# Hybrid decoder step: two of five expert value sums read the whole value table, and the order of work ahead of the first gather

## The reference, cut to what matters

```python
xn = rmsnorm(x); xr, yr, ca, cb, ga, gb = split(xn @ w_in)          # 2048 x 8192
branch_a = (rglru(conv4(xr)) * gelu(yr)) @ w_a                       # recurrence over time
branch_b = silu(layernorm(conv31(ca * sigmoid(cb)))) @ w_b           # 31 taps, 1024 channels
x = x + (sigmoid(ga) * branch_a + sigmoid(gb) * branch_b) @ w_out
# experts: 16384 of them, 8 heads, 16 of each head for each token
q = (rmsnorm(x) @ w_q).reshape(t, 8, 2, 128)
s1, s2 = q[:, :, 0] . keys1, q[:, :, 1] . keys2                      # 128 scores each
e, sv = top16 of (top16(s1) + top16(s2));  e = i1 * 128 + i2
w = softmax(sv) * gelu(u_tab[e] . xn)                                # one dot product of 2048 for each
x = x + sum over heads and k of w * v_tab[e]                         # u_tab, v_tab: 16384 x 2048
y = rmsnorm(x) * g_final
```

## Time and profile before

| | us |
|---|---|
| median of 3 runs | 4106.34 (4100.68 to 4108.57) |
| the profiled execution | 4110.75 |
| its span, first to last instruction | 4108.9 |

### The profile page before, as it was taken

The page is one execution under the profiler, slowest core; times in us unless marked ns, Lnnn a source line. Parts: engine busy times, 40 slices in busy tenths (PEclk is TensorE's granted clock), DMA queues, the critical chain, the costliest instruction groups (busy, mean ns, idle before and its releaser), DMA issues.

```text
span 4108.9 us, 35344 instructions
## 1 busy us (share of the span) xinstructions
PE 3168.1 (77%) x11808; PEld 1910.2 (46%) x11808; DVE 2447.8 (60%) x3360; ACT 556.5 (14%) x1113; POOL 1543.0 (38%) x1130
## 2 busy tenths in 40 slices
PE   6999899879878776857915777777777777776776
PEld 5999889775444443535502233232223232322322
DVE  2788810146787775784666565566556555656553
ACT  4444320110010000001000100010011001001100
POOL 2000000014554443552336455445445544554442
PEclk9999999889999998978968999999999999999999
DMA  4322367569999998896879999999999999999997
GB/s 122 89 85 84 104 215 242 190 244 344 391 380 387 385 392 343 333 385 253 342 263 406 409 416 421 421 403 421 414 416 417 422 415 415 418 421 412 422 412 306
DMA packets 406321, 1372.39 MB, mean 334 GB/s; under 512 B 24449, under 2 KB 264065, under 8 KB 264735
## 3 DMA queue, kind: packets, MB, share of 16 engines
q0 software_dynamic: 157584, 1145.05, 68.3%
q1 hardware_dynamic: 246382, 221.85, 16.9%
q10 hardware_dynamic: 2257, 4.40, 0.3%
HBM read 1363.20 MB, written 8.86 MB: 334 GB/s over the span
## 4 chain that ended last, share of the span: by engine, by line
DMA 43%; PE 29%; DVE 14%; issue 9%; POOL 4%; ACT 1%; SPq 0%; DVEq 0%; POOLq 0%; ACTq 0%
DMA region<-in_v_tab_dram,region 29%; DMA region<-in_u_tab_dram,region 13%; PE ps L1366 11%; PE ps L1547 6%; POOL region L527 4%; DVE region L1177 3%; PE ps L1349 3%; PE ps L1351 3%; PE ps L1350 3%; DVE region L1230 2%; DVE region L1168 1%; DVE region L1129 1%; DVE region L1126 1%; DVE region L1128 1%; DVE region L1125 1%
## 5 line engine op out<-in xcount | busy, mean ns | idle before, releaser
L1547 PE MATMUL ps<-region,region 128*128 128x512 f32 x3032 | 1429.1, 621 | 544.0 <-DMA region<-in_v_tab_dram,region 326.8
L1366 PE MATMUL ps<-region,region 128*128 128x160 f32 (+1 forms) x5120 | 1237.2, 404 | 190.4 <-DVE region L1065 57.3
L1230 DVE SCALAR_TENSOR_TENSOR region<-region,region 128x2048 f32<-128x2048 f32 x384 | 876.2, 2291 | 738.8 <-DMA region<-in_u_tab_dram,region 738.8
L527 POOL DMA_INDIRECT region<-in_v_tab_dram,region x544 | 764.3, 1405 | 1268.6 <-PE ps L1547 675.8
L1547 PEld LDWEIGHTS ps<-region,region 128*128 128x128 f32 x3032 | 575.8, 197 | 1397.4 <-issue 1304.3
L1366 PEld LDWEIGHTS ps<-region,region 128*128 128x128 f32 x5120 | 861.1, 196 | 558.9 <-issue 104.1
L527 POOL DMA_INDIRECT region<-in_u_tab_dram,region x544 | 740.7, 1362 | 794.3 <-DVE region L1158 341.0
L1177 DVE SCALAR_TENSOR_TENSOR region<-region,region,region 128x2048 f32<-128x2048 f32 x160 | 376.1, 2351 | 236.8 <-DMA region<-in_v_tab_dram,region 236.6
L1168 DVE SCALAR_TENSOR_TENSOR region<-region,region 128x2048 f32<-128x2048 f32 x160 | 365.3, 2285 | 22.8 <-DMA region<-in_u_tab_dram,region 22.8
L1349 PE MATMUL ps<-region,region 128*128 128x272 f32 x1024 | 297.4, 290 | 0.0
L1351 PE MATMUL ps<-region,region 128*128 128x272 f32 x1024 | 296.4, 289 | 0.0
(11 more groups left out here) (202 smaller groups left out, 1483.2 us busy)
## 6 DMA issues: line engine op xcount, KB each, us to landing
region<-in_w_in_dram SPq DMA_DIRECT2D x192, 512.0 KB
region<-in_w_out_dram SPq DMA_DIRECT2D x64, 512.0 KB
region<-in_w_q_dram SPq DMA_DIRECT2D x64, 512.0 KB
region<-in_w_a_dram SPq DMA_DIRECT2D x32, 512.0 KB
region<-in_w_b_dram SPq DMA_DIRECT2D x32, 512.0 KB
region<-in_u_tab_dram,region POOLq DMA_INDIRECT x544, 14.0
region<-in_v_tab_dram,region POOLq DMA_INDIRECT x544, 14.0
region<-in_x_prompt_dram SPq DMA_DIRECT2D x7, 1024.0 KB, 15.7
```

The source lines that it names most:

```text
L527: pool.indirect_dma_start(out=slot, out_offset=None, in_=rows_ap, in_offset=bass.IndirectOffsetOnAxis(ap=idx[:, k:k + 1], axis=0)).then_in ...
L1230: stt(out=u_b[s], in0=u_b[s], scalar=1.0, in1=xn_tile(UNITS_A + u), op0=ALU.mult, op1=ALU.mult, accum_out=dots[u % 2][:, k:k + 1]).then_in ...
L1366: last = mm(outs[n][:, 0:WIDTH[g]], wide[s][:, q, n * P:(n + 1) * P], rhs(k), start=(k == 0), stop=(k == n_k - 1))
L1547: last = mm(acc[n][:, b * 512:(b + 1) * 512], diag[:, m, :], v_b[s][:, b * 512:(b + 1) * 512], start=(m == 0), stop=(m == len(rows) - 1))
```

## The change

1. **Values of tiles 0 and 1 by the whole table.** The 256 value gathers of these tiles (256 MB) are gone. Instead the 128 x 128 weights of each token over (i2, i1) are built, and `v_tab` is read once, 128 chunks of 128 experts (1 MB each); each chunk is multiplied into both tiles: 2 x 4 matmuls of 128 x 128 by 128 x 512.
   - `split_experts` (DVE) splits the indices of a tile in two; `turn` (PE, 3 transposes) and `turned_copy` (ACT) put the 128 (head, k) of a token on the partitions.
   - 32 batches of 4 tokens for each tile: `first_ones` (DVE, 4 instructions: column equals i1, times weight), `second_ones` (ACT, 4 squares of (column - i2) and one Relu(1 - square)), `batch` (PE, 4 products 128 x 128 by 128 x 128), `keep_weights` (ACT, PSUM to SBUF: 512 columns, written 4 together, 128 apart; read 128 apart).
   - Tile 0's batches are spread over rows 136 to 251 of stage B; tile 1's stand at rows 258 to 265 (`BATCH_AT`), 4 at each. On ACT they stand ahead of the next unit's scores.
   - `SP` loads chunk c when chunk c - 2 has been used (2 buffers).
2. **Tile 2** is done last, on VectorE: dot product of row z, then value row z - 18, with 2 buffers for `u_tab` rows and 2 for `v_tab` rows (before: 4 and 4), beside the chunks.
3. **Values of stage A.** Of its 160 value rows 80 stay on VectorE, spread evenly behind the dot products (`VALUE_AT`); the other 80 go to TensorE with diagonal weights, spread over the first 224 rows of stage B (`ROW_AT`), with the 2 buffers of stage A. The last rows of stage A's list end with the queries: 18 rows for the 8 heads (before: 32, and 18 more for the lag behind them).
4. **Scores of group 1** are written to DRAM (3 MB, `scores_kept`) after the last head, since their place is needed; each unit's 128 KB come back through ACT's DMA queue.
5. **Ahead of the first gather:** the last chunk's 31-tap convolution is split by columns (`last_conv`): group 0's 128 prompt columns first, the other 384 in three parts among the norm and merges of group 0, ahead of `norm_mean(1)`; `gate_b(0, 1)` moves ahead of `norm_mean(1)`; the four sums of `xp` (L1074) stand behind `norm_scale(0)`; the clears behind `channels_out(0)` and `route(0)`; the score of group 0's head 0 right behind its own product; two clears on GpSimd at the start behind its first subtraction.

The diff, cut to its core:

```diff
+ROWS_W = 5 * TOPK
+ROWS_1, ROWS_B = 2 * P, 3 * P
+VALUE_AT = {V_LAG + v * (ROWS_A - V_LAG) // ROWS_W: v for v in range(ROWS_W)}
+ROWS_P = ROWS_A - ROWS_W
+ROW_AT = [m * (ROWS_1 - 2 * TOPK) // ROWS_P for m in range(ROWS_P)]
+BATCH = 4
+BATCHES = P // BATCH
+BATCH_AT = [[P + 8 + b * (P - 9) // BATCHES for b in range(BATCHES)],
+            [ROWS_1 + 2 + b // 4 for b in range(BATCHES)]]
...
-    return 142 + 4 * h, 146 + 4 * h
+    return 142 + 18 * h // HEADS, 142 + 18 * (h + 1) // HEADS
...
+            sp.wait_ge(v_used, ROWS_P)
+            for c in range(CHUNKS):
+                if c == 1:
+                    sp.wait_ge(built, 2 * BATCHES)
+                if c >= 2:
+                    sp.wait_ge(vt_used, c - 1)
+                sp.dma_start(v_t[c % 2], v_rows[c * P:(c + 1) * P, :]).then_inc(vt_landed[c % 2], 16)
...
+            for r in range(ROWS_1):
...
+                if r >= SLOTS:
+                    pool.wait_ge(dot_b, r - SLOTS + 1)
+                gather(u_rows, u_b[r % SLOTS], ub_landed[r % SLOTS], idx_all, ROWS_A + r)
+                for m, at_row in enumerate(ROW_AT):
+                    if at_row == r:
...
+                            pool.wait_ge(v_used, m - SLOTS_V + 1)
+                        value_row(ROWS_W + m)
+            for z in range(P + V_LAG + 1):
...
+                    pool.wait_ge(dot_b, r - 1)
+                    gather(u_rows, u_b[2 + z % 2], ub_landed[2 + z % 2], idx_all, ROWS_A + r)
+                v = z - V_LAG - 1
...
+                        pool.wait_ge(v_added, ROWS_W + v - SLOTS_V + 1)
+                    value_row(ROWS_A + v)
...
+            def second_ones(t, b):
+                n = t * BATCHES + b
+                if n >= 2:
+                    act.wait_ge(built, n - 1)
+                for q in range(BATCH):
+                    last = nc.scalar.activation(one_b[n % 2][:, q, :], count, ACT.Square, scale=-1.0,
+                                                bias=turned[:, 1, BATCH * b + q:BATCH * b + q + 1])
+                last.then_inc(b_square, 1)
+                act.wait_ge(b_square, n + 1)
+                nc.scalar.activation(one_b[n % 2], one_b[n % 2], ACT.Relu, scale=-1.0, bias=ones[:, 0:1]).then_inc(b_ones, 1)
...
+            def keep_weights(t, b):
...
+                act.wait_ge(built, n + 1)
+                if t == 0:
+                    nc.scalar.activation(wx[:, :, cols], src, ACT.Copy).then_inc(kept_w, 1)
+                else:
+                    nc.scalar.activation(wy[0][:, :, cols], src[:, 0:HALF], ACT.Copy)
+                    nc.scalar.activation(wy[1][:, :, cols], src[:, HALF:CHUNKS], ACT.Copy).then_inc(kept_w, 1)
...
             norm_center(0)
...
+            last_conv(0, 12, 0, NBT)
             norm_scale(0)
+            join_parts((0, 1, 2, 3))
+            last_conv(12, 18, 0, NBT)
             merge(0, 0)
             merge(0, 1)
+            last_conv(18, CW, 0, NBT)
...
+            for r in range(ROWS_B):
+                u, k = divmod(r, TOPK)
+                dot(r)
+                if k == 1:
+                    expert_weights(UNITS_A + u - 1)
+                if k == (12 if u == 2 * HEADS else 3) and u < UNITS_B - 1:
+                    route(UNITS_A + u + 1)
...
+                if r >= ROWS_1 + V_LAG:
+                    value_z(r - ROWS_1 - V_LAG)
...
+            for c in range(CHUNKS):
+                s = c % 2
+                pe.wait_ge(vt_landed[s], 16 * (c // 2 + 1))
+                for n in range(2):
+                    w = wx[:, c, :] if n == 0 else wy[c // HALF][:, c % HALF, :]
                     for b in range(4):
...
+                        last = mm(acc[n][:, b * 512:(b + 1) * 512], w, v_t[s][:, b * 512:(b + 1) * 512],
+                                  start=(c == 0), stop=(c == CHUNKS - 1))
```

More of the change, by code:

```diff
@@ L97, in steps_query @@
 def steps_query(h):
-    return 142 + 4 * h, 146 + 4 * h
-PE_ROWS = (tuple(range(TOPK)), tuple(k for k in range(TOPK) if k not in SHARED))
+    return 142 + 18 * h // HEADS, 142 + 18 * (h + 1) // HEADS
 class Steps:
@@ L576, in _ @@
[L576 to L588 removed]
+                    value_row(v)
@@ L843, in _, with build @@
+            def build(t, batches):
+                for b in batches:
+                    second_ones(t, b)
+                    if b > batches[0]:
+                        keep_weights(t, b - 1)
+                if batches:
+                    keep_weights(t, batches[-1])
             for j in range(DC):
@@ L1241, in normalised @@
+            def normalised(tiles, n, g):
                 dve.wait_ge(rms_sqrt, n)
@@ new lines, in _ @@
+            for r in range(ROWS_1):
+                for m in range(ROWS_P):
+                    if ROW_AT[m] == r:
+                        value_row(m)
+                if r == SPLIT_AT[0]:
+                    turn(0)
+                for b in range(BATCHES):
+                    if BATCH_AT[0][b] == r:
+                        batch(0, b)
+                if r == FOLD_AT - 3:
+                    pe.wait_ge(acc_read, 2)
+                    for b in range(4):
+                        last = mm(acc[0][0:TS, b * 512:(b + 1) * 512], sel[:, 1, 0:TS], xf[1][:, b * 512:(b + 1) * 512],
+                                  start=True, stop=True)
+                    last.then_inc(fold_done, 1)
```

493 lines of the change are left out of this document (314 added, 179 removed).

## The result

| | us |
|---|---|
| changed kernel, median of 4 runs | 4193.48 (4190.24 to 4202.32) |
| kernel before, on the same chip, median of 4 runs | 4107.45 (4100.68 to 4111.97) |
| ratio | 1.0214, 95% interval 1.0197 to 1.0231 |

The change makes the kernel 2.1% slower, 86 us. The forecast was 4055 us: the sign is wrong and the time is 138 us off. The profiled execution of the changed kernel took 4202.32 us, its span 4200.5.

The account below looks back on a forecast made before the run. Taken as bound by gathers (DMA) in stage B and the branches, by PE in the queries. Sum: 936 + 560 + 230 + 182 + 15 + 944 + 103 + 1063 + 21, 1.85 outside the span: 4056, forecast 4055 us; range 3885 to 4150.

Parts of the forecast that it names:

- step 5: Stage B, tiles 0 and 1: 16 units of 59 us (bounds 53 and 66), 944 us, ending at 2867.
- step 7: Chunks beside tile 2: 1063 us, rows at 8.8 us (bounds 7.5 and 10.5), bound by tile 2's two-buffer loop.
- Step 1: Ahead of the first gather: 3 us off the start of group 1 (936), 11 for the gather.
- Step 2: Group 1's branches: 669 becomes 560 us, pairs of 70 us (bounds 66 and 76).
- Step 3: Output blocks: 268 becomes 230 us (bounds 215 and 250).
- Step 4: Queries: 190 becomes 182 us, the 59 us behind them go, late scores add 15; stage B starts at 1923.
- Step 6: Building tile 1's weights ahead of the chunks: 103 us, 2.8 us a batch (bounds 2.5 and 4.5).
- rival C: Tile 1's build: strided PSUM copies cost three times 0.8 us, build 51 us longer, kernel 4107 us; chance 0.05.
- Step 8: End, from tile 2's last value row: 21 us (15 to 30), against 12.8 before.
- A: Stage B: the DMA queue stays full, units 55 us, tile 2's stretch 980 us, kernel 3909 us; chance 0.3.
- B: Tile 2 beside the chunks: the two-buffer loop takes 10.2 us a row, +87 us, kernel 4143 us; chance 0.2.
- a lasting fall to 1.2 GHz: PE beside tile 2: long waits for chunks drop its clock from 2.4 GHz, a chunk then taking 13.8 us.

Follow-up runs that it names:

- the halves: Changed kernel with each 1 MB value-table chunk loaded and multiplied as two column halves of 512 KB: 4176.99 us, 1.0177 of before.
- the best version: Changed kernel with value gather first, route in three parts, chunks in halves, and tile 0's batches at each unit's 9th, 11th, 13th and 15th row: 3984.11 us.
- the two orders: Changed kernel with the value gather issued ahead of the expert-row gather beside tile 2, and each stage B route in three parts: 4100.97 us.
- all three edits: Changed kernel with value gather first beside tile 2, stage B routes in three parts, and chunks loaded in column halves: 4026.65 us, 0.9801 of before.

## Why the prediction was wrong

The largest misses of the sum are step 5 (+84 us) and step 7 (+63).

**Step 1** (start, 3 us): the start of group 1 moved by 2 us (937.1 for 939). "First gather near 845" was wrong: I followed the moved work to the indices and not to the semaphore that releases the gather, whose instruction waits for ScalarE.

**Step 2** (branches): right, the window 936 to 1500 answers to 560 us. **Step 3** (output blocks): 250 in place of 230, at the upper bound. I had left 24 us above the floors of two engines and read 30 for before; by the prediction's own figures that was 27 above the DMA engines' 241 and 62 above PE's 206, and now it is 44 above both. Neither PE (179.4 busy) nor the DMA engines (0.86) is full. No run took this apart, and the cause stays open. **Step 4** (queries): 185 for 182, so that they ended at 1935, 27 us later than forecast, and PE's wait of 51 us behind them is gone, as forecast. The first unit of stage B then took 83.7 us, 21 more than the others; DVE waits 19.9 us for the first scores to come back from DRAM. I had allowed 15 for that ahead of stage B; it came behind its first rows, and so stage B started only 12 us late.

**Step 5** (units of 59): the mechanism was the right one, the queue that drains during a route, and the run with the route in three parts shows it (57.8). What failed is its size, and with it the sentence on what hides ACT's batches. The idle time is 7.5 us (12% of 62.8) for 6; the refill is slower than I took from the earlier trace rows, where the issue takes 0.94 us: behind a route DVE is busy without a break and the issues on GpSimd take about 2 us. The transfers took some 55 us for 52.8, since in tiles 0 and 1 the engines moved 355 GB/s at a share of 0.88, 403 for a full share, and not 417. And the order of the batches, which I had called covered ("What hides ACT's batches: 4 of 2.7 us for each unit, on an engine busy a tenth"): ACT is idle, but it is idle because it waits, and what stands behind its wait is needed by PE and then by GpSimd. A low busy share was taken for availability. In tile 1 it costs 4.6 us a unit once the route is cut (63.7 to 59.1). The first unit is 25 us of the 84, the other seven of tile 0 are 25, tile 1's eight 34.

**Step 6** (build): 91 us for 103; a batch is 2.46 us for 2.8 (32 of 2.8 are 90 us, not the 91 of the sum), and rival C (the strided copies are dear) is refuted. Tile 0's copies, by form:

```profile
L931 ACT ACTIVATE region<-ps 128x512 f32<-128x512 f32 x32 | 19.1, 597 | 236.3 <-PE ps L1758 236.3
```

512 columns read 128 apart take 0.60 us, while 544 contiguous ones took 0.63; tile 1's copies of 256 take 0.37. The rule of the Trainium skill, "Advanced Engine Details and Errata", section Memory Cachelines, on every two consecutive elements doesn't show in these copies on ScalarE.

**Step 7** (tile 2), 63 us. What failed is the sentence "both are shorter than what I hold for the bound": I priced the chunks by PE's work, 128 x 6.9, and never worked out their own loop of two buffers, though I had done so for the rows. They come every 8.4 us, last 1076 us instead of 900, and so stand beside the rows to the end: the 12 rows at 7.2 don't exist (+21), 98 rows at 8.98 take 880 us and not 860 (+20), the last 18 values 15 us more, the first rows 7.

The run with the halves shows what that error is worth. Its chunks last 897 us, as forecast, and its last 16 rows, behind the chunks, come 7.1 us apart (no route falls in them). The stretch is then 1095.7 us, 31 less than in the changed kernel (the medians differ by 16), and 33 us above the forecast stay: the rows beside the chunks come 9.1 us apart, the first rows take 7 us more and the last values 8. Nor was the 8.8 us of a row forecast for the right reasons. Without chunk loads a row takes 7.90 us, where my loop gave 7.2 (6.7 and 0.5 for the route); the loads add 1.1 us, where I had 1.6. Two errors of opposite sign brought the forecast near the measured 8.98, which is luck.

**Step 8**: 20.3 us for 21.

Of the rivals, A (the queue stays full, 3909) was approached once the order of the work was changed: the best version takes 3984 us, with a share of 0.94 to 1.02 outside the build. B had the right sign and a right place, with a price per row that is not what was measured (10.2; 8.98). Its sum is off too: 26 rows at 7.2 in place of 12 are 101 us more, so B stands at 4157 and not 4143. The kernel came out on B's side because tiles 0 and 1 were late and the chunks slow as well. The two-sided range, 3885 to 4150, missed by 43 us, since it added no lateness in tiles 0 and 1 to lateness in tile 2; both happened. Both stages had lost buffers (4 + 4 became 4 + 2, then 2 + 2) while the forecast valued the bytes saved at the full rate. That this is the common reason is argued and not shown: no run gave the buffers back.

## What to carry to other kernels

Bytes saved in a stage that is bound by DMA are worth their time only if the transfers left are still asked for early enough; after such a change work out for every stream (each with its own buffers) the loop release, issue, transfer, use, and compare it with the shared bound. Two loops of nearly the same length hide each other, so an edit to one that brings little is no evidence against it: open both. An in-order queue that waits is not idle in the sense of free: place work that others need behind the point at which the wait ends, as one line did here for 43 us.

## What the runs showed of the hardware

**A gather's issue on GpSimd takes longer beside a busy VectorE.** Of 832 issues in the changed kernel, the 363 in whose first 0.94 us DVE was busy for a tenth or less have a median of 0.94 us; the 339 in which it was busy for nine tenths or more (mostly dot products of two f32 operands in SBUF) have a median of 2.24 us, about a dot product's 2.29. In the kernel before the medians are 0.94 and 2.24 too, while stage B ran at a full share; behind a route it sets the pace. The Trainium skill, "SBUF — State Buffer", section SBUF: two separate sides, has the port pair that DVE and GpSimd share as an exclusive lock, held for the whole instruction, which fits; that the lock is the cause no run isolated.

**A busy DMA engine isn't always at its full rate.** GB/s over share, beside tile 2: without chunk loads 268 at 0.72, which is 372 for a full share; in the changed kernel 360 at 0.93, 387; with the halves 386 at 0.98, 394; with the two orders (whole chunks) 416 at 1.01, 412; with all three edits 414 at 1.02, 406. Before, with gathers alone, it was 417 at 1.01. Gathers alone give the lowest and the highest of these, so the mix alone doesn't decide; a busy engine's rate was lower where the share was below 1.

**PE's clock** was mostly at its upper level beside tile 2 in the changed kernel, granted 0.96 on average, although PE waits 18 us at times; a lasting fall to 1.2 GHz, which I had named as what would make me altogether wrong, didn't come there. In tiles 0 and 1, where PE works 47% of the time, the clock goes to and fro between the two levels, 0.73 on average.
